# Two moves in VectorE's program: four block sums one product later at the middle of an MLP, and a square sum and a split change places

## What is computed

```python
x = x + mixed @ w_out[l]
h = _rmsnorm(x, ln_mlp_g[l])
x = x + jnp.square(jax.nn.relu(h @ w_mlp_up[l])) @ w_mlp_down[l]
```

## Time and profile before

| | |
|---|---|
| median of three runs | 2309.3 us |
| lowest and highest | 2307.2 and 2312.32 us |
| span of the profiled execution | 2308.3 us |
| TensorE busy | 2254.4 us, 98% of the span |
| VectorE busy | 1619.5 us, 70% |
| GpSimd busy | 1109.7 us, 48% |
| ScalarE busy | 792.1 us, 34% |
| chain that ended last | TensorE 91%, VectorE 5%, ScalarE 1%, DMA 1% |

### The profile page before, as it was taken

The page is one execution under the profiler, slowest core; times in us unless marked ns, Lnnn a source line. Parts: engine busy times, 40 slices in busy tenths (PEclk is TensorE's granted clock), DMA queues, the critical chain, the costliest instruction groups (busy, mean ns, idle before and its releaser), DMA issues.

```text
span 2308.3 us, 29200 instructions
## 1 busy us (share of the span) xinstructions
PE 2254.4 (98%) x10818; PEld 1868.1 (81%) x10818; DVE 1619.5 (70%) x1974; ACT 792.1 (34%) x1068; POOL 1109.7 (48%) x853
## 2 busy tenths in 40 slices
PE   7999999999999999999999999899999999999998
PEld 5678888888888899887878888788888887779886
DVE  7899999986778454546686666777777601578777
ACT  4312242123333356222343333443443102444423
POOL 4236553333323256333478888898885433300130
PEclk9999999999999999999999999999999999999999
DMA  4121223533332422444244444744431311431231
GB/s 155 37 83 64 64 91 113 166 134 117 110 128 83 128 74 61 151 159 150 101 167 152 151 151 150 279 174 153 155 119 51 137 55 37 119 126 47 66 110 73
DMA packets 92560, 267.71 MB, mean 116 GB/s; under 512 B 8785, under 2 KB 25305, under 8 KB 87193
## 3 DMA queue, kind: packets, MB, share of 16 engines
q1 hardware_dynamic: 75376, 200.04, 26.4%
q10 hardware_dynamic: 17064, 66.08, 8.1%
HBM read 183.51 MB, written 81.80 MB: 115 GB/s over the span
## 4 chain that ended last, share of the span: by engine, by line
PE 91%; DVE 5%; ACT 1%; issue 1%; DMA 1%; SPq 0%; ACTq 0%; DVEq 0%
PE pair L1113 44%; PE pair L1453 25%; PE pair L1610 4%; PE pair L1361 3%; PE pair L1579 2%; PE pair L1566 1%; PE pair L1131 1%; PE pair L1339 1%; PE pair L1281 1%; PE pair L1328 1%; PE pair L1330 1%; DVE tsp L2661 1%; PE pair L1555 1%; PE pair L1552 1%; PE pair L1554 1%
## 5 line engine op out<-in xcount | busy, mean ns | idle before, releaser
L1113 PE MATMUL pair<-actA,w_hi 128*128 128x512 f32 x2016 | 624.1, 391 | 2.1 <-issue 2.1
L1113 PEld LDWEIGHTS pair<-actA,w_hi 128*128 128x128 f32 x2016 | 377.5, 188 | 80.8 <-ACT sq L1748 2.9
L1113 PE MATMUL pair<-actA,w_lo 128*128 128x512 f32 x1008 | 392.9, 390 | 0.0
L947 POOL TENSOR_TENSOR pad<-pad 128x1 f32<-128x1 f32 x111 | 31.5, 284 | 707.4 <-PE pair L1113 619.8
L1453 PE MATMUL pair<-tring,wsp 128*128 128x512 f32 x1344 | 307.5, 391 | 7.2 <-DVE tring L2734 5.7
L1453 PEld LDWEIGHTS pair<-tring,wsp 128*128 128x128 f32 x1344 | 253.1, 189 | 61.3 <-issue 8.0
L951 POOL TENSOR_TENSOR w_lo<-raw,w_hi 128x1024 fp32r<-128x1024 f32 (+1 forms) x111 | 258.0, 2324 | 8.9
L1113 PEld LDWEIGHTS pair<-actA,w_lo 128*128 128x128 f32 x1008 | 189.7, 188 | 39.9
L1453 PE MATMUL pair<-tsp,wsp 128*128 128x512 f32 x768 | 184.0, 391 | 4.1 <-DVE tsp L2661 2.0
L2702 DVE TENSOR_TENSOR xB<-pair,xB 128x1024 f32<-128x1024 f32 x112 | 136.4, 1220 | 71.2 <-PE pair L1453 70.9
L2389 DVE MAX8 top<-pen 128x8 f32<-128x384 f32 (+5 forms) x192 | 171.7, 894 | 6.4
(11 more groups left out here) (412 smaller groups left out, 4380.1 us busy)
## 6 DMA issues: line engine op xcount, KB each, us to landing
raw<-w_in SPq DMA_DIRECT2D x80, 512.0 KB, 3.6
wraw<-w_pair SPq DMA_DIRECT2D x32, 1024.0 KB, 7.3
staged<-hid_d SPq DMA_DIRECT2D x56, 512.0 KB, 3.4
proj<-stage ACTq DMA_DIRECT2D x40, 512.0 KB, 2.7
hid_d<-hsum SPq DMA_DIRECT2D x16, 1024.0 KB, 5.0
gates<-proj ACTq DMA_DIRECT2D x18, 512.0 KB, 5.2
raw<-w_out SPq DMA_DIRECT2D x16, 512.0 KB, 3.6
hid_d<-hid SPq DMA_DIRECT2D x16, 512.0 KB, 2.8
```

The source lines that it names most:

```text
L1113: last = nc.tensor.matmul(pair[par][:, cols], w[:, slot, wk], x[:, cols], start=(k == 0 and i == 0), stop=(k == kt - 1 and i == 2))
```

## The change

Two places of VectorE's program are written in another order; no instruction is added or taken away.

```diff
             last_sums((1, 3))
+            sum_lo(1, 3)
             add_square(NT - 1)
             dve.wait_ge(ss_sum, NT + 1)
-            sum_lo(1, 3)
             event(1)
...
-                if p == "P1" and st <= N_PAIR:
+                if p == "P1" and st < N_PAIR:
                     unit_sums(st - 1)
                 for j in range(N_SPLIT):
                     if T_TURN[j] == i:
                         split_lo(j)
+                if i == NO[N_PAIR, "P5"]:
+                    unit_sums(N_PAIR - 1)
```

## The result

Seven runs of each kernel on the same chip, taken in turns: 2308.15 us before (2304.85 to 2312.32), 2317.27 us after (2312.0 to 2318.49). The ratio is 1.0032, with a 95% interval of 1.0022 to 1.0042: the change makes the kernel slower by 7.4 us, 5.1 to 9.7 (the ratio applied to the median before; the medians themselves lie 9.1 us apart). The forecast was 2315.5 us, 0.27% slower. The profiled execution of the changed kernel is the slowest of its seven, 2318.49 us.

A forecast was written before the change was run, and what follows sets the result against it. Bound: TensorE, with run 123 held by a chain from VectorE's last sum through step 18's weights. Terms 0, 0, +4.45 and +1.7 gave +6.15 us: span 2314.5, median 2315.5 us, range 2308.5 to 2318.5.

The forecast's parts named there:

- What sets the time of run 123: MLP: an unbroken chain of 27.07 us from last sum over store, loads and step 18's weights; run 123 starts 4.45 later.
- Its corollary: MLP: taking the 4.98 us gap away altogether would give nothing, as run 123 hangs on the chain.
- the first gap: MLP: TensorE's 4.98 us idle time moves one matmul run later, to before run 116, and is 5.6 us; net 0.
- The size of the shift: VectorE's last sum, alternating with GpSimd, moves from 1474.59 to 1479.05: a loss of 4.45 us, bounds 0 to 6.7.
- rival B: Step 18's weights land when they did before through unseen slack, run 123 unmoved: not slower, 2309.3 us; chance 0.20.
- The clock behind the second gap: TensorE after the 5.1 us gap before run 123: a stretch at half clock, +1.7 us, bounds 0 to 3.4.
- rival A: As forecast, but without half clock after the gap before run 123: +4.45 us, 2313.8 us; chance 0.13.
- The first place: Split put ahead of the square sum: TensorE's 0.57 us wait goes, run 4 waits for event(1) instead; 0 us.
- The sum: Whole kernel: all terms together add 6.15 us to the span of 2308.3, giving 2314.5; as median 2315.5 us.

The follow-up runs named there:

- run 123: Not a follow-up: TensorE's matmul run after the second MLP gap; starts at 1501.66 in the kernel before, 1505.78 in the changed kernel.
- run 122: Not a follow-up: TensorE's last matmul run ahead of the second MLP gap; ends 32.88 us after event(112) started before, 33.47 in the changed kernel.
- second place alone: Kernel before with only the four block sums moved one down product later, the split left in its old order; ratio 1.0034.
- store held back: Kernel before, VectorE's order untouched; SyncE holds the store of the four sums until a later split, that for run 116, is done; ratio 1.0035.
- one split ahead: Changed kernel with the four sums one step earlier, behind the first of the two splits that preceded them; ratio 1.0016.
- run 116: Not a follow-up: TensorE's matmul run in the MLP that follows the first gap in the changed kernel, starting at 1479.92.
- the first two kernels with the weights first: Kernel before and changed kernel, each with SyncE issuing step 18's weights ahead of the store of the four sums; ratios to the kernel before 0.9995 and 1.0001.
- run 0: Not a follow-up: TensorE's matmul run that opens the stretch up to event(112), which takes 318.09 us in the kernel before.
- run 4: Not a follow-up: TensorE's matmul run at the first place that needs event(1); starts at 1161.31 in the kernel before.

## Why the prediction was right

**What sets the time of run 123.** The prediction said that the gap of 1.11 us, not that of 4.98 us, decides, as it ends a chain from the last sum over the store, the loads and the weights of step 18. Shown: cutting the chain at the weights takes the loss away, and delaying the store alone makes it. Its corollary, that taking the first gap away altogether would give nothing as long as the chain stands, was not run. What speaks for it is the table: the end of run 122 varies by 1.3 us in the kernels with the chain, and run 123 keeps its distance from the store.

**The size of the shift.** Counted: 4.45 us, from VectorE and GpSimd in turns. Measured: the store moved from 6.95 to 11.36 us behind the start of event(112), 4.41, and run 123 by 4.43. The steps were 1.77, 1.65, 1.63 and 1.64 us for the four sums where 1.69 was counted for each, and 1.21 us for the two splits ahead of them, the first of which took 2.28 us before. The prediction's four other marks were the store at 1479.1 (1478.71), L862 at 1483.3 (1483.20), the weights' issue at 1486.5 (1486.34) and their arrival at 1500.1 (1499.82), and the measured ones are to be read with the 0.32 us by which this profile is early. The load took 13.4 us, where it took 13.6 before: rival B, a flight shorter by 4.4 us, did not happen. The Trainium skill ("DMA: Bandwidth & Descriptors", "Queues, rings and completion order") says that each DMA engine takes descriptors in the order of its ring; that agrees with a flight of 13.3 to 13.6 us wherever 4 MB of loads were issued just ahead (before, changed, second place alone, store held back, one split ahead), where the median of the 32 loads of a step's weights is 7.3 us on the page of either profile.

**The first gap.** Forecast 5.6 us before run 116, measured 5.56. Its half clock cost some 1.7 us and was absorbed, as in the kernel before: the seven runs show as 20.90 us, where 7 * 2.72 = 19.06 and some 0.16 is the end of the last run (a run shows as 2.88 us and the next starts 2.72 us later).

**The clock behind the second gap.** The direction was right and the size low: the term was 1.7 us and measured 277.26 - 275.00 = 2.26 us. The clock stayed low for more of TensorE's work there (0.50 from run 123's start to 1510, 0.67 from 1510 to 1511, some 4.9 us of work) than behind the first gap of the kernel before (from 1476.94 to 1480.3, some 3.4 us), from which the term had been taken. Filling the gap gave 2.3 us back. One argument for this term was weaker than it looked: against rival A the prediction held that a gap of 1.76 us had a half clock too. That gap is in all ten profiles with the same length, and the clock fell to 0.50 behind it in three of them (before and the first two kernels with the weights first), not in the other seven. This is the changed kernel:

```profile
1066.07 0.73 PE L1131 MATMUL pair<-actA,w_hi 128*128 128x512 f32 x2 [1.76 <-DVE actA L2279]
```

```profile
1067.00:1068.00 1.00, 1.00 (x6) 0.81 (x5) 1.00 (x2) 0.26 (x1) 0.00 (x0) 1.00 1.02 401
```

So whether a half clock follows a gap as short as that can differ from one execution to the next, and a single profile does not settle it. Behind each gap of 4 us or more in this place, in the ten profiles, it was there.

**The first place.** Forecast 0, measured 1.0001 alone, and 0.1 us more from run 0 to event(112). The wait moved ahead of run 4 as said.

**The sum.** 6.15 us forecast, 6.70 us in the profile's own stretch, 7.4 (5.1 to 9.7) by the runs. What the runs have over the profile's 6.70 is inside the interval and needs no cause.

## What to carry to other kernels

A gap in the bottleneck engine that is followed by a second one is worth nothing until the second one is explained: look there for what ends last, and follow it back to where it starts, here to a store that a queue has put ahead of an unrelated load. When an instruction is moved, its consumers on the DMA queue move with it, and so does all that is queued behind them in order; the cheap remedy was to issue the load whose own condition is already met (the weights, at 1471.17) ahead of the store that has to wait (1479.01). A releaser that a view names can be one that merely ended at the same moment; compare it with the bank's and the tile's last reader before believing it.

## What was not expected of the hardware

In the middle of the MLP the second gap of these profiles, before run 123, was 2.58 us (one split ahead), 4.31 (second place alone), 4.66 (store held back) and 4.95 us (changed), and TensorE's clock was at 0.50 behind each of them; it was at 1.00 behind the one of 1.11 us (before). Of the gap of 1.76 us at an earlier place, the same in all ten profiles, three had the half clock and seven did not.

What the half clock costs does not follow the length of the gap. It follows how long TensorE works at 0.50 once it has gone on, and is nearly half of that time: 1.55 us for some 3.3 us of such work (behind 4.66 us), 1.62 for 3.4 (behind 2.58), 2.26 for 4.9 (behind 4.95) and 2.82 for 6.0 (behind 4.31), each cost against 275.00 us for the same runs. In the one profile in which TensorE was kept busy with products that nobody needs, it stayed at 1.00.
